# Two-block expert pairs moved from turns 2 and 4 to turns 6 and 11 of a mixture-of-experts loop

## The reference

```
g_idx = argmax(x @ w_group + b_group)                # 1 of 4 groups
top_p, top_i = top_k(softmax(e_logits[group]), 2)    # 2 of its 8 experts
eid = g_idx * 8 + top_i                              # 640 x 2 = 1280 assignments to 32 experts
def expert_block(xb, e):
    return (silu(xb @ w1[e]) * (xb @ w3[e])) @ w2[e] # w1, w3: 1024x512, w2: 512x1024, float32
out[token] += gate * expert_block(...)
```

## Time and profile before

| | us |
|---|---|
| median of 3 timed runs | 1290.64 (1287.18 to 1291.11) |
| profiled execution, its own time | 1281.86 |
| its span, first to last instruction | 1280.0 |
| PE busy | 1100.2 (86%) |
| DVE busy | 448.2 (35%) |
| ACT busy | 313.4 (24%) |
| POOL busy | 96.9 (8%) |

### The profile page before, as it was taken

One profiled execution on the slowest core, in us unless ns is written; L12 is line 12 of the kernel. 1 busy time (PEld: TensorE's weight loads), 2 busy tenths in 40 slices (PEclk: granted clock), 3 DMA queues, 4 the chain that ended last, 5 costly groups with the idle time before them and its releaser, 6 DMA issues. The chain is left out here.

```text
span 1280.0 us, 16697 instructions
## 1 busy us (share of the span) xinstructions
PE 1100.2 (86%) x6380; PEld 720.7 (56%) x6381; DVE 448.2 (35%) x1030; ACT 313.4 (24%) x720; POOL 96.9 (8%) x146
## 2 busy tenths in 40 slices
PE   5999889999888979998889949999999988777870
PEld 4978556887556867997658743444444432323320
DVE  5432644634865455404562251111111111111106
ACT  7130644302567344304353200000000000000002
POOL 2110002000010000000000001011001100000003
PEclk9999999999999989999999969999999998899895
DMA  8213422234308946415172399999799999999966
GB/s 284 68 43 142 165 77 74 72 114 170 127 17 332 421 146 230 165 66 197 70 291 106 151 421 425 427 373 428 326 427 427 429 427 427 427 428 428 428 289 246
DMA packets 75324, 329.98 MB, mean 258 GB/s; under 512 B 18258, under 2 KB 19043, under 8 KB 62979
## 3 DMA queue, kind: packets, MB, share of 16 engines
q1 hardware_dynamic: 64690, 302.95, 59.0%
q0 software_dynamic: 7696, 18.40, 3.8%
q10 hardware_dynamic: 2880, 7.87, 1.6%
HBM read 294.52 MB, written 43.54 MB: 264 GB/s over the span
## 5 line engine op out<-in xcount | busy, mean ns | idle before, releaser
L1964 PE MATMUL bank<-ring,xT 128*64 128x512 f32 x1152 | 265.6, 618 | 34.4 <-DMA ring<-in_w 32.9
L1964 PEld LDWEIGHTS bank<-ring,xT 128*64 128x64 f32 x1152 | 97.3, 142 | 199.9 <-issue 180.7
L1981 PE MATMUL bank<-ring,hT 128*64 128x512 f32 x576 | 127.6, 594 | 17.8 <-ACT hT L2016 9.6
L2179 DVE TENSOR_TENSOR sg<-bank,sg 128x512 f32<-128x512 f32 x18 | 12.4, 692 | 276.4 <-PE bank L1964 276.4
L1981 PEld LDWEIGHTS bank<-ring,hT 128*64 128x64 f32 x576 | 47.6, 137 | 85.3 <-issue 85.3
L214 DVE TENSOR_TENSOR ring_r<-ring,ring_r 128x512 fp32r<-128x512 f32 x128 | 80.3, 683 | 19.9 <-ACT ring_r L209 19.7
L255 PE MATMUL bank<-ring_r,nH_r 128*128 128x512 f32 x200 | 80.0, 400 | 0.6 <-PE bank L257 0.3
L2012 ACT ACTIVATE sg<-bank 128x512 f32<-128x512 f32 x18 | 10.7, 597 | 280.5 <-PE bank L1964 280.5
L257 PE MATMUL bank<-ring_r,nT_r 128*128 128x512 f32 x200 | 78.4, 392 | 0.0
L256 PE MATMUL bank<-ring_r,nH_r 128*128 128x512 f32 x200 | 78.1, 391 | 0.0
L209 ACT CAST ring_r<-ring 128x512 fp32r<-128x512 f32 x128 | 70.3, 618 | 28.3 <-PEq L1661 18.5
(11 more groups left out here) (403 smaller groups left out, 1797.2 us busy)
## 6 DMA issues: line engine op xcount, KB each, us to landing
ring<-in_w SPq DMA_DIRECT2D x96, 2048.0 KB, 28.8
expert_rows<-rozero SPq DMA_DIRECT2D x1, 18432.0 KB, 54.7
ring<-in_w_in SPq DMA_DIRECT2D x6, 2048.0 KB, 11.2
ring<-in_cache_mem_k SPq DMA_DIRECT2D x8, 1024.0 KB, 7.3
ring<-in_cache_mem_v SPq DMA_DIRECT2D x8, 1024.0 KB, 10.1
ring<-in_cache_fox_k SPq DMA_DIRECT2D x8, 512.0 KB, 6.7
ring<-in_cache_fox_v SPq DMA_DIRECT2D x8, 512.0 KB, 7.8
ring<-in_cache_diff_k SPq DMA_DIRECT2D x8, 512.0 KB, 6.0
```

The costliest lines, as they stand in the source:

```text
L1964: ins = nc.tensor.matmul(ps[2 + i][64 * x:64 * x + 64, :], xT[:, k, 64 * x:64 * x + 64], w(2 * i + x, t)[:, k, :], start=k == 0, stop=k == ...
L1981: ins = nc.tensor.matmul(ps[5 + half][64 * x:64 * x + 64, :], hT[:, k, 64 * x:64 * x + 64], w(4 + x, t)[:, k, half * 512:(half + 1) * 512] ...
L2179: nc.vector.tensor_tensor(hh[:, :], ps[3][:, :], sg[:, :], ALU.mult).then_inc(hid_done, 1)
```

## The change

A tuple `TURN_OF_RANK` gives each pair-rank its turn, in place of a formula that alternated light and heavy pairs from the front.

```
+TURN_OF_RANK = (6, 11, 3, 8, 13, 4, 9, 1, 14, 7, 12, 5, 10, 2, 15)
...
-    turns = (PAIRS - FIXED // 2)
-    for r in range(turns):
-        at = R_PLACE + FIXED + 2 * min(2 * r + 1, 2 * (turns - 1 - r))
-        cst[:, at:at + 2] = FIXED + 2 * r + np.arange(2)
+    for r, at in enumerate(TURN_OF_RANK):
+        cst[:, R_PLACE + 2 * at:R_PLACE + 2 * at + 2] = FIXED + 2 * r + np.arange(2)
```

More of the change, by code:

```diff
@@ L56 @@
 FIXED = 2
+TURN_OF_RANK = (6, 11, 3, 8, 13, 4, 9, 1, 14, 7, 12, 5, 10, 2, 15)
+assert sorted(TURN_OF_RANK) == list(range(FIXED // 2, PAIRS))
 R_GROUP, R_EXPERT, R_HALF, R_CAP, R_BLOCK, R_PLACE, R_SLOT, R_TILE, R_P, R_SIZE = 0, 4, 12, 44, 53, 92, 128, 256, 266, 272
```

## The result

| | before | after |
|---|---|---|
| median of 9 timed runs each, us | 1287.02 (1283.22 to 1291.11) | 1279.42 (1275.32 to 1283.03) |
| ratio, 95% interval | | 0.9935 (0.9915 to 0.9956) |
| profiled execution: own time, span | 1281.86, 1280.0 | 1279.55, 1277.7 |

The kernel got faster by 0.65% (0.44 to 0.85%), that is 8.4 us by the ratio. With 9 runs, the median of before is 1287.02 and not the 1290.64 of the first three. So the forecast time of 1279.1 fits partly by luck: the forecast gain of 11.5 us (0.9%) lies a little outside the interval.

A forecast was written before the change was run, and what follows sets the result against it. The prediction took the last weight matrix's landing, behind a stream full except for two gaps, as the bound. Closing both saves 11.5 us, all other terms 0: 1290.64 becomes 1279.1 us, range 1274 to 1286.

The forecast's parts named there:

- What bounds the loop: Expert loop: its end is set by the last matrix's landing, behind a weight stream full except at two places.
- Instructions at nothing: Expert loop: same table size, 18 blocks, 90 loads and 1280 gathered rows, so the change costs 0 us in instructions.
- The issue times: Weight loads: turn 4's first can be issued at 825 us, turn 6's first at 871.8.
- The reserve behind a two-block pair: Loads of turns 8 and 13: 17 us in hand, 14 left after a load's start, so no new gap, 0 us.
- The closed gaps: Weight stream before turns 4 and 6: two empty stretches vanish, 11.4 us by landings, 11.7 by bytes, taken as 11.5.
- the first gap: Weight stream before turn 4's first load, held up by turn 2's second block: 2.9 us empty, to be closed.
- the second: Weight stream before turn 6's first load, held up by turn 4's second block: 8.5 us empty, to be closed.
- My count by bytes: Both empty stretches, priced by their GB/s against the full 428: 4.0 and 7.8 us, together 11.7.
- The count by landings: Both empty stretches, priced by time between landings less 5.2 us a load: 2.9 and 8.5, together 11.4 us.
- The clock at nothing at the end: TensorE at half clock after waits: a few more 3 us losses from turn 5 on, none costing time at the end.
- 7 us of cover in turn 15: Turn 15: TensorE wants w2 7 us before it lands, so the last `down` again starts on a landing.
- TensorE catching up: After the two-block turns 6 and 11: turn 7 runs without a wait, turn 14's w2 is wanted at 1192.5, lands at 1193.0.

The follow-up runs named there:

- The run with 10 fillers: Changed kernel plus 10 unused matmuls on the identity before the wait for w3 in every odd turn; ratio to before 0.9933 (0.9916 to 0.995).

## Why the prediction was right, and where its sum was off

**What bounds the loop** was right: the landing of the last weight matrix, behind a stream that is full except where a two-block pair holds up the loads of two turns later. Moving just those pairs there and back moved the gain with them.

**Instructions at nothing, light pairs' order at nothing**: right within what the same pair of runs can tell, which is 0.2 to 0.3%.

**The issue times** were right to a microsecond or so. Forecast for turn 4's first load were 825, which is 53.8 us after the first matmul, and 871.8 for turn 6's, 100.4 after it; measured 53.9 and 100.5. The reserve behind a two-block pair was given as 17 us: turn 8's first load was issued at 963.1, with turn 7's last landing at 981.0, so 18.

**The closed gaps, 11.5 us**: this is the term that was mis-sized. The last landing came 8.5 us sooner (463.9 against 455.4 us from the first matmul). With the first gap alone (turns 2 and 11) it came 2.5 us later than without any, for the 2.9 worked out, so the larger error lies in the second: some 6 us for 8.5. My count by bytes takes the stream's mean rate, and with it the idle of all 16 engines. The profiles compare like this, each row by one profile; the idle is 32 x (1 - rate/428) summed over low slices, and the cost is against 455.3, the mean of the three profiles with no low slice (455.4, 455.7, 454.7). The share is that of the 16 engines in the 10 us before the last landing:

| two-block turns | low slices, GB/s | idle by bytes, us | first matmul to last landing, us | cost, us | share |
|---|---|---|---|---|---|
| 2 and 4 (before) | 373, 326 | 11.7 | 463.9 | 8.6 | 0.94 |
| 2 and 4 (others as after) | 404, 336 | 8.7 | 462.1 | 6.8 | 0.90 |
| 2 and 11 | 381 | 3.5 | 457.8 | 2.5 | 0.85 |
| 6 and 7 | 377 | 3.8 | 455.7 | 0.4 | 0.98 |
| 4 and 6; 6 and 11 | none | 0 | 454.7 to 455.7 | 0 | 0.71 to 0.74 |

The shares of the second and the third row:

```profile
1226.90:1236.90 10.00, 9.60 (x40) 4.06 (x40) 0.68 (x1) 0.00 (x0) 0.00 (x0) 0.83 0.90 373
```

```profile
1223.80:1233.80 10.00, 9.64 (x33) 3.17 (x33) 0.00 (x0) 0.00 (x0) 0.00 (x0) 0.72 0.85 352
```

What is lost is always less than the idle by bytes, and in the fourth row it is not to be told from nothing, since the gapless profiles differ by 1.0 us themselves. My reading, argued and not shown engine by engine: engines with less row traffic run ahead of the others. In a gap they wait first, and that wait costs nothing, because without a gap they have it at the end. The shares bear this out: every kernel with a gap ends fuller than the ones without. The difference between 0.94 and 0.72 is 2.2 us of mean idle moved from the gaps to the end. From turn 1's first load to the last landing the changed kernel also moved 0.27 MB more (201.81 against 201.54), which is 0.6 us. Of this 0.17 MB are rows: the last turn now holds 35 rows, not 77, so more of the results are stored before the last landing. 11.7 - 2.2 - 0.6 is 8.9, where 8.5 was measured. The same sum against the changed kernel gives 6.5 us for the second row (measured 6.7), 1.3 for the third (2.4) and 1.0 for the fourth (0.3), all within about 1 us. The count by landings, 11.4, erred too. It charges a full load's step of 5.2 us, part of it row traffic, and rows that move during a gap are done with afterwards. That too is argued from the table, not measured by itself.

**The clock at nothing at the end**: wrong by 1.5 us in this profile. I had read from one profile that the last turn's w3 products run at 7.09 us, and so put the term at nothing. In the changed kernel TensorE waited 3.33 us for w3, the granted clock fell (0.83 in the mean of the last 10 us and 0.58 in 1222 to 1226 us, near the lower level of 0.50, against 1.00 in before's), and the 32 products took 8.78 us, so that the last `down` was late by 1.6. A last `down` that begins after the last landing was one of the prediction's own signs of being wrong. I had counted 7 us of cover in turn 15, from the time at which TensorE is done with turn 14. The cover that counts runs from w3's own landing: 1222.14 + 7.09 + 2.51 for turning and hand-over (1233.43 - 1222.14 - 8.78) is 1231.74, and w2 lands at 1231.8. That is no cover at all, so every loss of clock in the w3 products shows at the end. The run with 10 fillers gives that back. But it is not the new order that does it: with the pairs put back to turns 2 and 4 the last `down` was also 1.7 us behind its landing, w3 at 8.78. Of the ten profiles without fillers that end on the stream, eight show the last `down` 1.4 to 2.6 us behind the last landing, with w3 products of 8.6 to 9.7 us, and only before's and the one without row traffic 0.1. So the 7.09 that I read from one profile of before was not typical. If before mostly has the lag as well, the term cancels in medians; the timed gain of 8.4 us, near the 8.5 of the landings, fits that, but more profiles of before would have to show it. The Trainium skill's page "TensorE: Matmul & The Clock Gate", section "HAM oscillation — how this bites in real kernels", which says that DMA waits keep throwing the array back to its low clock, bears on the end of the loop more than I allowed: I held against it that the last products ran at 7.09.

**TensorE catching up**: right for turns 7 and 12. In turn 14 it waited 2.29 us for w2, where 0.5 was worked out, so it was in time with 2 us to spare.

**The rivals**: no gap came back, a slower stream in the new order did not show (425 to 430 GB/s), and two blocks stood where the ranking puts them.

## What to carry to other kernels

In a loop that streams weights into two sets of buffers, a turn with twice the compute holds up the loads of two turns later; it costs only if the queue of loads already issued runs empty in the meantime. Here that queue was shortest in the first turns and longest in the last; but in the last turns TensorE has no time left to catch up, so the place for such a turn is in between. Read the queue from issue-to-landing times: 8 us meant an empty stream, 15 us and more a full one. And price an idle stretch of the DMA by a kernel in which it is moved or closed: the mean rate said 11.7 us and the steps between landings 11.4, and it was worth 8.5.

## What the hardware showed that I had not expected

The DMA share can fall to 0.66 while loads keep landing every 5.2 us (two-block turns 6 and 7), and the 16 engines come apart through 10 MB of row gathers and scatters among 190 MB of loads: share 0.99 in the last 10 us without them, 0.72 with them, 0.50 with the same rows on other partitions, which alone put the last landing 4.4 us later (1283.08 against 1279.42 us timed). A matmul of the identity with itself, 128x128 in float32, shows as two records and took 0.236 us in a row of 20 (4.73 / 20) and 0.25 in a row of 10 (2.50 / 10).
